# Expert passes of two sizes instead of eight, with TensorE's passes in a loop

## The chip, the cores and the metric

The kernel runs on one core of a Trainium2 chip. The metric is the device time of one execution in microseconds (us). It is one inference step of a two-layer decoder trunk, in float32 throughout, written directly for the engines with semaphores: every engine has its own instruction stream, and nothing reorders it.

## The reference, cut to what matters

288 tokens (256 of a prompt, 8 sequences of 4 new ones) go through two layers. Each layer mixes tokens by three recurrent branches and then has a feed-forward part: dense in layer 0, and a mixture of experts in layer 1. Only the latter is touched here.

```python
def swiglu(h, w1, w3, w2):
    return (jax.nn.silu(h @ w1) * (h @ w3)) @ w2

def moe_swiglu(h, router, w1, w3, w2):
    logits = (h @ router).astype(jnp.float32)
    top_v, top_i = lax.top_k(logits, TOP_K)            # 2 of 8
    probs = jax.nn.softmax(top_v, axis=-1)
    gate = jnp.sum(jax.nn.one_hot(top_i, N_EXPERTS) * probs[..., None], axis=-2)
    for e in range(N_EXPERTS):
        out = out + gate[..., e:e + 1] * swiglu(h, w1[e], w3[e], w2[e])
```

A token has 1024 features, an expert's hidden width is 2816. So 576 pairs of token and expert fall on eight experts, 72 on average.

## The kernel before, in words

**Passes.** An expert's tokens are gathered into a block of columns, and one pass multiplies this block with the expert's weights. A pass has a fixed number of columns, its cap. `CAPS` gives the caps in the order of the passes 0 to 7: 91, 88, 73, 85, 76, 82, 79, 70, together 644. The experts are ranked by how many tokens they got, on VectorE (DVE) at run time, and `PASS_OF_RANK` says which pass the expert of a rank takes; so the fullest gets 91 columns and the emptiest 70. Tokens beyond a cap go to extra passes of the last cap. Passes 0 to 6 are the fixed ones (`FIXED` = 7); pass 7 and all extra ones are turns of a loop whose count is read from a register (`passes`, L2722).

**Routing.** L2875 to L2882 make the rank (`order`), the cap of each expert (`cap_of`) and its pass (`pass_of`); after them DVE scales the gathered tokens (`take_gathered`, L2869), for which TensorE (PE) waits before pass 0. The rest of the routing runs beside pass 0.

**A pass on PE** (`expert`, L2681). First the up part: 44 slabs of weights (128 x 1024, 512 KB each, w1 and w3 in turn), each 8 matmuls in two halves of 64 rows (`narrow_products`, L454). It is a loop of five turns over eight slabs (L2685) and four slabs behind it. Then a transposed scatter matrix (L2648) and the gathering of the next pass's tokens (L2619, L2626). Then the down part, a loop of four turns (L2696), each over two output blocks of three slabs (L2661; 512, 512 and 384 KB), followed by the adding of earlier results to all 288 tokens (L2672) and transposes (L2679). ACT takes silu of the w1 product (L2744), DVE multiplies it by the w3 product (L2958), ACT takes the down products (L2748).

**PE's code.** Passes 0 to 6 are seven copies of this code, made by a Python loop, with their own caps; pass 7 is an eighth copy, inside the register loop. The two inner loops are loops of the engine in each copy. ACT and DVE have one loop of seven turns and one for the rest (L2788, L2965), and work on the whole width `CAP` in all passes.

**Loads.** SyncE's queue (SPq) issues all weight loads in one order. The up slabs have a ring of eight places (`RING`, issued at L441), the down slabs a ring of six (L2525). In each pass SPq loads the first six down slabs of that pass as the last six of the pass before are used, then up slabs 8 to 43, each when slab n - 8 is used, then the first eight up slabs of the next pass, then down slabs 6 to 23. So eight up slabs and six down slabs at most lie ready. A pass loads 44 x 512 KB and 24 down slabs, 34.6 MB in all.

**Elsewhere.** The retention stage of each layer has a PE loop of four turns over a long body (L678).

Of the kernel before, what the change touches and what calls it, by code (L numbers as in the profile page):

```python
# [19 lines left out]
ALU = mybir.AluOpType  # L20
# [17 lines left out]
FF = 2816  # L38
FT = FF // 128
NE = 8  # L40
CAP, CAP_STEP = 91, 3
FIXED = NE - 1
PASS_OF_RANK = (0, 1, 3, 5, 6, 4, 2, 7)
CAPS = [CAP - CAP_STEP * PASS_OF_RANK.index(q) for q in range(NE)]
LAST_CAP = CAPS[FIXED]
OVERFLOWS = 7
MAXP = 1 + OVERFLOWS
NFF = NE + 1
# [58 lines left out]
def constants():  # L107
# [51 lines left out]
    c["tie"] = np.tile(np.concatenate([[1e6], -np.arange(1.0, NE)]), (128, 1))  # L159
    c["pass_of_rank"] = np.tile(np.array(PASS_OF_RANK, float), (128, 1))  # L160
    off, at = 0, {}
# [59 lines left out]
def build(nc, xT_in, w_mix, w_lora, w_rank, w_gkup, vec_in, vecf_in, router_in, w_ff, s_ret, s_gla, s_rw,  # L221
# [50 lines left out]
    def settle(eng):  # L272

        eng.sem_inc(settled, 1)
# [2184 lines left out]
    def experts(nc, block, sig, layer, merge, rs):  # L2460
# [12 lines left out]
        key, above, order, cap_of, excess = w(NE), w(NE, NE), w(NE), w(NE), w(NE)  # L2473
# [25 lines left out]
        def count(p, per, k):  # L2499

            i, done = p
            return i * per + (done * per + k)
# [65 lines left out]
        def _(pe):  # L2568
# [39 lines left out]
            def keep_busy(n, unused):  # L2608

                for k in range(n):  # L2610
                    mm(unused[:, 0:T], ones, xT[:, k, :], start=True, stop=True)

            def gather_tokens(n, cap):

                pe.wait_ge(sig("picked"), n)
                for j in range(2):
                    for r in range(4):
                        rows = slice(NS * r, NS * r + NS)
                        mm(HG[r][:, CAP * j:CAP * j + cap], htok2[rows, j, :], gather[rows, 2, 0:cap], start=(j == 0),  # L2619
                           stop=False)  # L2620
                for r in range(4):
                    for j in range(2):
                        k = 4 * j + r
                        for i in range(2):
                            for c in range(2):
                                last = mm(HG[r][64 * c:64 * c + 64, CAP * j:CAP * j + cap],  # L2626
                                          htok[:, i, 128 * k + 64 * c:128 * k + 64 * c + 64], gather[:, i, 0:cap],
                                          start=False, stop=(j == 1 and i == 1))
                    last.then_inc(sig("hg_ps"), 1)

            def up(p, cap, n, turn):

                i, done = p
                s = n % RING
                per = len(range(s, UP_SLABS, RING))
                fill = fills_before(layer, s) + fills(len(STREAM), s) + done * per + n // RING + 1
                pe.wait_ge(slab_in[s], turn * 16 + (i * (per * 16) + fill * 16))
                pe.wait_ge(sig("w3_free" if n % 2 else "w1_free"), turn * (RING // 2) + count(p, FT, n // 2 + 1))
                if n in (2, 3):
                    pe.wait_ge(sig("oT"), count(p, KT, n - 1))  # L2640
                narrow_products(pe, s, bank[n % 4][:, 0:cap], hg[:, :, 0:cap])

            def scatter_matrix(p):

                pe.wait_ge(sig("gated"), count(p, 1, 1))
                pe.wait_ge(sig("w3_free"), count(p, FT, FT + 1))
                for i, (a, n) in enumerate(TILES):
                    last = nc.tensor.transpose(SC[0:CAP, a:a + n], gated[0:n, i, :], ident[0:n, 0:n])  # L2648
                last.then_inc(sig("scatter_ps"), 1)

            def down(p, cap, t, m):

                i, done = p
                pe.wait_ge(sig("oT"), t * 2 + count(p, KT, m + 1))
                for c in range(3):
                    d = 3 * m + c
                    pe.wait_ge(down_in[d], t * 16 + (i * 64 + (done * 64 + 16)))
                    n = 6 if c == 2 else KT
                    for k in range(n):
                        for h in range(2):  # L2660
                            last = mm(DOWN[m][64 * h:64 * h + 64, 0:cap], down_ring[:, d, k, 64 * h:64 * h + 64],  # L2661
                                      hid[:, KT * c + k, 0:cap], start=(KT * c + k == 0), stop=(KT * c + k == FT - 1))
                    last.then_inc(slab_done, 1)
# [12 lines left out]
            def to_tokens(p, t, m):  # L2676

                pe.wait_ge(sig("oT"), t * 2 + count(p, KT, m + 3))
                nc.tensor.transpose(OTOK[m][0:CAP, 0:128], oT[:, m, :], ident).then_inc(sig("otok_ps"), 1)  # L2679

            def expert(p, cap, next_cap):  # L2681

                pe.wait_ge(sig("hg"), count(p, 1, 1))
                settle(pe)
                with pe.Fori(0, UP_SLABS // RING) as g:  # L2685
                    for n in range(RING):
                        up(p, cap, n, g)
                for n in range(UP_SLABS // RING * RING, UP_SLABS):
                    up(p, cap, n, 0)
                scatter_matrix(p)  # L2690
                pe.wait_ge(sig("otok"), count(p, KT, 2))
                pe.wait_ge(sig("added"), count(p, KT, 2))
                gather_tokens(count(p, 1, 2), next_cap)
                pe.wait_ge(sig("w3_free"), count(p, FT, FT + 2))
                settle(pe)
                with pe.Fori(0, KT // 2) as t:  # L2696
                    for m in range(2):
                        down(p, cap, t, m)
                    for m in range(2):
                        add_up(p, t, m)  # L2700
                    for m in range(2):
                        to_tokens(p, t, m)
# [10 lines left out]
            sample_tokens()  # L2713
            keep_busy(3, bank[7])
            pe.wait_ge(sig("htok"), 1)
            gather_tokens(1, CAPS[0])
            pe.wait_ge(sig("zeroed"), 1)
            keep_busy(1, bank[3])
            for q in range(FIXED):
                expert((0, q), CAPS[q], CAPS[q + 1])  # L2720
            rest = passes(pe)
            with pe.Fori(0, rest) as i:  # L2722
                expert((i, FIXED), LAST_CAP, LAST_CAP)
            LAST = rest * KT + FIXED * KT
# [81 lines left out]
        def _(dve):  # L2806
            tt, ts, stt = nc.vector.tensor_tensor, nc.vector.tensor_scalar, nc.vector.scalar_tensor_tensor
# [3 lines left out]
            def then(ins):  # L2811

                steps[0] += 1
                ins.then_inc(sig("route"), 1)
                dve.wait_ge(sig("route"), steps[0])
# [59 lines left out]
            then(stt(out=key, in0=total, scalar=float(NE), in1=cst("tie"), op0=ALU.mult, op1=ALU.add))  # L2875
            then(tt(above, rep(key, 1, NE), column_of(key, NE), ALU.is_gt))
            then(reduce(order, above, X, ALU.add))
            ts(cap_of, order, float(-CAP_STEP), float(CAP), ALU.mult, ALU.add)
            then(tt(above, rep(cst("iota8"), 1, NE), column_of(order, NE), ALU.is_equal))
            then(tt(above, above, rep(cst("pass_of_rank"), 1, NE), ALU.mult))  # L2880
            reduce(pass_of, above, X, ALU.add)
            then(tt(excess, total, cap_of, ALU.subtract))  # L2882
            take_gathered(0)

# [4 lines left out]
            nc.vector.reciprocal(gate2[:, 0, :], den)  # L2889
            ts(turns, beyond, float(LAST_CAP), None, ALU.is_ge)  # L2890
            for c in range(1, -(-(T - LAST_CAP) // LAST_CAP)):
                then(stt(out=npass, in0=excess, scalar=float(c * LAST_CAP), in1=npass, op0=ALU.is_gt, op1=ALU.add))
                if c > 1:
                    stt(out=turns, in0=beyond, scalar=float(c * LAST_CAP), in1=turns, op0=ALU.is_ge, op1=ALU.add)
            tt(gate2[:, 1, :], gate2[:, 0, :], ex, ALU.mult)
# [5 lines left out]
            then(stt(out=move, in0=move, scalar=float(CAP), in1=cap_of, op0=ALU.mult, op1=ALU.subtract))  # L2901
            then(stt(out=turns, in0=turns, scalar=float(CAP - LAST_CAP), in1=rep(move, 1, 3), op0=ALU.mult, op1=ALU.add))
            then(tt(turns, turns, over, ALU.mult))
# [47 lines left out]
            def expert(p):  # L2951

                for f in range(FT):
                    dve.wait_ge(slab_done, count(p, FF_SLABS, FF0 + 2 * f + 2))
                    if f == 0:
                        settle(dve)
                    dve.wait_ge(sig("w1_free"), count(p, FT, f + 3))
                    tt(hid[:, f, :], bank[(2 * f + 1) % 4][:, 0:CAP], act1[:, f % 2, :],  # L2958
                       ALU.mult).then_inc(sig("w3_free"), 1)
                    choose(p, f)  # L2960
                take_gathered(count(p, 4, 4))
                for m in range(KT):
                    add_up(p, m)
# [346 lines left out]
```

## Time and profile before

| | us |
|---|---|
| median of 3 runs | 2512.42 (2511.38 to 2513.73) |
| the profiled execution, its own time | 2513.11 |
| its span, first to last instruction | 2511.3 |
| PE busy | 2442.6 (97%) |
| DVE busy | 1291.6 (51%) |
| ACT busy | 609.9 (24%) |

The profile is one execution. Its page gives the busy time of each engine, the span in 40 slices with what the DMA engines moved, the DMA queues, the chain of work that ended last, and groups of instructions by line. Its own time is 0.7 us above the median. The expert passes fill the time from about 1766 to 2498 us. A busy PE says only that matmuls were under way; whether they came as fast as they could is read from the distance between equal events.

### The profile page before, as it was taken

How to read it: one execution, taken by the hardware profiler on the slowest of the kernel's cores; microseconds unless marked ns; L12 is line 12 of the kernel's file. 1: busy time of each engine (PE TensorE's matmuls, PEld its weight loads, DVE VectorE, ACT ScalarE, POOL GpSimd, SP SyncE). 2: the span in 40 equal slices, each digit the busy share in tenths (PEclk: the TensorE clock that was granted, in tenths of full speed). 3: DMA queues.
4: the chain of work that ended last, by engine and by line, in shares of the span. 5: the costliest groups of instructions: out<-in, count | busy, mean ns of one | idle time of the engine just before them, and what ended most of it. 6: DMA issues, size and time to landing. Idle time of an engine off the chain costs nothing. (4 is left out here: it accounts for less than half of the span.)

```text
span 2511.3 us, 103490 instructions
## 1 busy us (share of the span) xinstructions
PE 2442.6 (97%) x45930; PEld 2040.3 (81%) x45930; DVE 1291.6 (51%) x3328; ACT 609.9 (24%) x1798; POOL 0.2 (0%) x4
## 2 busy tenths in 40 slices
PE   9999999999999999999999999999999999999997
PEld 7987666666699999998766666678999899888986
DVE  7666666666686676756576666667311111111111
ACT  2233333433311101233333334421111111111111
POOL 0000000000000000000000000000000000000000
PEclk9999999999999999999999999999999999999999
DMA  6334442222243454333353222234899999999997
GB/s 248 111 136 161 151 133 88 83 83 79 99 154 136 153 173 144 128 124 139 129 168 129 84 78 77 83 112 154 341 342 390 393 392 370 402 372 374 402 388 274
DMA packets 146091, 500.85 MB, mean 199 GB/s; under 512 B 18784, under 2 KB 23520, under 8 KB 143360
## 3 DMA queue, kind: packets, MB, share of 16 engines
q1 hardware_dynamic: 145792, 496.44, 54.7%
q8 instruction: 239, 3.92, 0.6%
q14 instruction: 60, 0.49, 0.1%
HBM read 476.08 MB, written 20.29 MB: 198 GB/s over the span
## 5 line engine op out<-in xcount | busy, mean ns | idle before, releaser
L301 PE MATMUL psum<-hT,ring 128*64 128x144 f32 (+1 forms) x4568 | 457.4, 346 | 3.7 <-DVE hT L2421 1.7
L454 PE MATMUL psum<-work,ring 128*64 128x91 f32 (+7 forms) x11264 | 422.0, 234 | 15.7 <-issue 7.3
L454 PEld LDWEIGHTS psum<-work,ring 128*64 128x64 f32 x11264 | 404.7, 136 | 33.3 <-issue 23.8
L301 PEld LDWEIGHTS psum<-hT,ring 128*64 128x64 f32 x4568 | 293.3, 137 | 96.2 <-issue 12.1
L2958 DVE TENSOR_TENSOR work<-psum,work 128x91 f32<-128x91 f32 x176 | 44.6, 253 | 365.4 <-PE psum L454 365.2
L2661 PE MATMUL psum<-work,proj 128*64 128x91 f32 (+7 forms) x5632 | 208.9, 234 | 10.6 <-issue 9.2
L2661 PEld LDWEIGHTS psum<-work,proj 128*64 128x64 f32 x5632 | 202.3, 137 | 16.1 <-issue 10.3
L1767 ACT ACTIVATE work<-psum 128x256 f32<-128x256 f32 (+4 forms) x320 | 104.1, 362 | 349.7 <-PE psum L1678 84.8
L301 PE MATMUL psum<-work 128*64 128x144 f32 (+4 forms) x2096 | 154.1, 282 | 4.3 <-DVE work L1258 3.6
L301 PE MATMUL psum<-y_ret,work 128*64 128x144 f32 x2400 | 156.3, 286 | 0.5 <-DVE y_ret L531 0.5
L301 PEld LDWEIGHTS psum<-y_ret,work 128*64 128x64 f32 x2400 | 148.7, 137 | 0.9 <-issue 0.9
L2949 DVE TENSOR_TENSOR xT<-xT,psum 128x288 f32<-128x288 f32 x64 | 29.1, 455 | 228.6 <-PE psum L2672 227.6
L301 PEld LDWEIGHTS psum<-work 128*64 128x64 f32 (+2 forms) x2096 | 121.3, 136 | 30.6 <-issue 11.3
L2744 ACT ACTIVATE work<-psum 128x91 f32<-128x91 f32 x176 | 43.5, 247 | 377.5 <-PE psum L454 377.5
L301 PE MATMUL psum<-y_ret,ring 128*64 128x144 f32 (+1 forms) x1280 | 126.8, 332 | 2.5 <-ACT work L1767 2.5
L301 PEld LDWEIGHTS psum<-y_ret,ring 128*64 128x64 f32 x1280 | 79.5, 137 | 18.4 <-ACT work L1767 4.5
L323 PE MATMUL psum<-hT,ring 128*128 128x288 f32 x252 | 72.8, 408 | 0.0
L2748 ACT ACTIVATE work<-psum 128x91 f32<-128x91 f32 x64 | 15.9, 248 | 228.1 <-PE psum L2661 228.1
L1563 PEld LDWEIGHTS psum<-work 64*64 64x64 f32 x1408 | 47.3, 134 | 29.4 <-issue 17.7
L546 DVE TENSOR_TENSOR y_gla<-psum,y_gla 128x288 f32<-128x288 f32 x72 | 33.0, 458 | 72.8 <-PE psum L301 72.2
L301 PE MATMUL psum<-hT,work 128*64 128x144 f32 x928 | 68.8, 287 | 0.0
L518 DVE TENSOR_TENSOR work<-ring 128x512 f32<-128x512 f32 (+1 forms) x90 | 54.7, 608 | 19.0 <-PE psum L301 19.0
(513 smaller groups left out, 3733.5 us busy)
## 6 DMA issues: line engine op xcount, KB each, us to landing
ring<-w_ff_dram SPq DMA_DIRECT2D x424, 512.0 KB, 7.3
ring<-w_mix_dram SPq DMA_DIRECT2D x256, 512.0 KB, 4.1
proj<-w_ff_dram SPq DMA_DIRECT2D x128, 512.0 KB, 5.3
proj<-w_ff_dram SPq DMA_DIRECT2D x64, 384.0 KB, 5.6
work<-s_gla_dram SPq DMA_DIRECT2D x8, 1024.0 KB, 5.3
gla_s_out<-work SPq DMA_DIRECT2D x8, 1024.0 KB, 4.7
work<-s_ret_dram SPq DMA_DIRECT2D x8, 512.0 KB, 5.4
ret_s_out<-work SPq DMA_DIRECT2D x8, 512.0 KB, 3.0
```

What stands on the lines that cost most here:

```text
L301: last = nc.tensor.matmul(out[64 * c:64 * c + 64], weights[:, 64 * c:64 * c + 64], x, start=start, stop=stop)
L323: mm = (in_halves if self.narrow else nc.tensor.matmul)(out, ring[:, s, k, :], rhs[:, k, :], start=(k == 0), stop=(k == KT - 1))
L454: mm = nc.tensor.matmul(out[64 * c:64 * c + 64], ring[:, s, k, 64 * c:64 * c + 64], rhs[:, k0 + k, :], start=(k0 + k == 0), stop=(k0 + k = ...
L518: op.tensor_tensor(s1, a21, a22, ALU.add).then_inc(sig("wsum"), 1)
L546: nc.vector.tensor_tensor(c[:, 1:3, :], two(LAST_TWO[side]), c[:, 5:7, :], ALU.add).then_inc(sig("outer"), 1)
L1563: last = mm(unit(half(W, r), c), half(AT, 1 - r)[:, c], half(X, 1 - r)[:, c], start=True, stop=True)
L1767: return nc.scalar.activation(out, in_, func, **kw)
L2661: last = mm(DOWN[m][64 * h:64 * h + 64, 0:cap], down_ring[:, d, k, 64 * h:64 * h + 64], hid[:, KT * c + k, 0:cap], start=(KT * c + k == 0) ...
L2744: ac(act1[:, f % 2, :], bank[2 * f % 4][:, 0:CAP], ACT.Silu).then_inc(sig("w1_free"), 1)
L2748: ac(oT[:, m % 2, :], DOWN[m % 2][:, 0:CAP], cp).then_inc(sig("oT"), 1)
L2949: tt(xT[:, k, :], xT[:, k, :], ADD[m % 2][:, 0:T], ALU.add).then_inc(sig("added"), 1)
L2958: tt(hid[:, f, :], bank[(2 * f + 1) % 4][:, 0:CAP], act1[:, f % 2, :], ALU.mult).then_inc(sig("w3_free"), 1)
```

## The change

The caps become two: 88 for passes 0, 2, 4, 6 and 76 for passes 1, 3, 5, 7, together 656 columns. The four fullest experts take the passes of 88, the others those of 76. The width on which ACT, DVE and the gather tables work (`CAP`) falls from 91 to 88. On PE the seven copies become a loop of three turns over two passes (88 and 76), one copy for pass 6, and the register loop for pass 7 and the rest as before. The routing gets the cap by a comparison and a multiplication, and one more small addition that must end before the next step. The loads, ACT's and DVE's loops stay as they are.

```diff
-CAP, CAP_STEP = 91, 3
+CAP, LAST_CAP, LARGE = 88, 76, 4
 FIXED = NE - 1
-PASS_OF_RANK = (0, 1, 3, 5, 6, 4, 2, 7)
-CAPS = [CAP - CAP_STEP * PASS_OF_RANK.index(q) for q in range(NE)]
-LAST_CAP = CAPS[FIXED]
+PASS_OF_RANK = (0, 2, 4, 6, 1, 3, 5, 7)
...
-            gather_tokens(1, CAPS[0])
+            gather_tokens(1, CAP)
             pe.wait_ge(sig("zeroed"), 1)
             keep_busy(1, bank[3])
-            for q in range(FIXED):
-                expert((0, q), CAPS[q], CAPS[q + 1])
+            with pe.Fori(0, LARGE - 1) as i:
+                expert((i * 2, 0), CAP, LAST_CAP)
+                expert((i * 2, 1), LAST_CAP, CAP)
+            expert((0, FIXED - 1), CAP, LAST_CAP)
             rest = passes(pe)
...
-            ts(cap_of, order, float(-CAP_STEP), float(CAP), ALU.mult, ALU.add)
+            ts(cap_of, order, LARGE - 0.5, float(LAST_CAP - CAP), ALU.is_gt, ALU.mult)
...
             reduce(pass_of, above, X, ALU.add)
+            then(ts(cap_of, cap_of, float(CAP), None, ALU.add))
             then(tt(excess, total, cap_of, ALU.subtract))
             take_gathered(0)
```

## Rows read from the trace of the kernel before

**Rows 1.** The page: span, busy time of engines, DMA in 40 slices, the up products.

```profile
span 2511.3 us, 103490 instructions
...
PE 2442.6 (97%) x45930; PEld 2040.3 (81%) x45930; DVE 1291.6 (51%) x3328; ACT 609.9 (24%) x1798; POOL 0.2 (0%) x4
...
DMA  6334442222243454333353222234899999999997
...
L454 PE MATMUL psum<-work,ring 128*64 128x91 f32 (+7 forms) x11264 | 422.0, 234 | 15.7 <-issue 7.3
```

**Rows 2.** Busy time by stretch, each from one scatter matrix to the next.

```profile
core 0: us, PE busy (x) PEld busy (x) DVE busy (x) ACT busy (x) POOL busy (x), PEclk, DMA share, GB/s
1826.70:1920.30 93.60, 92.07 (x2237) 88.23 (x2235) 13.72 (x41) 11.96 (x42) 0.00 (x0) 1.00 0.97 364
1920.30:2009.80 89.50, 87.01 (x2240) 79.70 (x2236) 13.71 (x41) 12.18 (x42) 0.00 (x0) 1.00 1.00 385
2009.80:2097.80 88.00, 86.20 (x2238) 81.55 (x2236) 13.71 (x41) 12.02 (x42) 0.00 (x0) 1.00 1.01 397
2097.80:2189.80 92.00, 87.34 (x2238) 80.57 (x2236) 13.72 (x41) 12.07 (x42) 0.00 (x0) 1.00 0.99 378
2189.80:2280.90 91.10, 85.18 (x2238) 80.63 (x2236) 13.72 (x41) 12.47 (x42) 0.00 (x0) 1.00 1.00 383
2280.90:2370.50 89.60, 87.69 (x2238) 81.21 (x2236) 13.71 (x41) 11.60 (x41) 0.00 (x0) 1.00 1.00 383
2370.50:2459.00 88.50, 83.46 (x2238) 75.93 (x2236) 13.71 (x41) 11.99 (x42) 0.00 (x0) 1.00 1.01 391
```

**Rows 3.** Timeline of ACT, passes 1 and 4: start, duration, what, [idle before].

```profile
1902.28 0.25 ACT L2744 ACTIVATE work<-psum 128x91 f32<-128x91 f32 x1 [2.18 <-PE psum L454]
...
2150.86 0.25 ACT L2744 ACTIVATE work<-psum 128x91 f32<-128x91 f32 x1 [1.86 <-PE psum L454]
...
2165.71 0.25 ACT L2744 ACTIVATE work<-psum 128x91 f32<-128x91 f32 x1 [2.32 <-PE psum L454]
...
2175.95 0.25 ACT L2744 ACTIVATE work<-psum 128x91 f32<-128x91 f32 x1 [2.32 <-PE psum L454]
```

**Rows 4.** Timeline of PE, down turns of passes 1 and 4.

```profile
1938.78 1.14 PE L2672 MATMUL psum<-work 91*64 91x288 f32 x8
...
1946.97 1.14 PE L2672 MATMUL psum<-work 91*64 91x288 f32 x8
...
2207.73 1.14 PE L2672 MATMUL psum<-work 91*64 91x288 f32 x8
...
2215.09 1.14 PE L2672 MATMUL psum<-work 91*64 91x288 f32 x8
```

**Rows 5.** Timeline of PE where it stops in passes 5, 3 and 7.

```profile
2223.86 4.91 PE L454 MATMUL psum<-work,ring 128*64 128x82 f32 x130
2230.20 4.72 PE L454 MATMUL psum<-work,ring 128*64 128x82 f32 x126 [1.43 <-issue]
2236.62 5.61 PE L454 MATMUL psum<-work,ring 128*64 128x82 f32 x149 [1.70 <-issue]
...
2107.13 3.02 PE L2661 MATMUL psum<-work,proj 128*64 128x85 f32 x77 [1.93 <-issue]
...
2469.19 3.96 PE L2661 MATMUL psum<-work,proj 128*64 128x70 f32 x74 [2.32 <-issue]
```

**Rows 6.** DMA queues: all of 140 to 229 us, then of the seven stretches.

```profile
q1 hardware_dynamic: 3406, 11.03, 34.4%
...
q1 hardware_dynamic: 68288, 241.33, 99.4%
q8 instruction: 36, 0.59, 0.4%
```

**Rows 7.** Retention loop: one turn by busy time, and its branches (first, last start).

```profile
168.00:199.10 31.10, 31.10 (x518) 27.64 (x516) 20.57 (x44) 10.76 (x21) 0.00 (x0) 1.00 0.38 135
...
L678 PEldq COMPARE_BRANCH  x8: 76/219/238, 136.3 to 1219.5; - x8
```

## The prediction

> **What bounds the kernel now.** I read the page first, then the expert passes by stretch, then single events of PE, ACT and the queues.
>
> The page [rows 1] shows PE busy for 97% of the span, so time follows PE unless PE is itself held to another's pace. The DMA line tells where that may be: it stands at 8 and 9 tenths from about 1757 us on, which are the expert passes, and far lower before. 11264 up products are 8 times 1408, so eight passes ran and no extra one.
>
> By stretch, each the down part of one pass and the up part of the next [rows 2], a stretch takes 88.0 to 93.6 us, and the DMA share is 0.97 to 1.01 in all. They carry 34.6 MB each at 364 to 397 GB/s. With 91 columns then 88 the rate is lowest and the time longest; where a small cap comes in, the rate rises and the time hardly falls. So there are two limits.
>
> ACT's silu comes once per two up slabs, so the distance of two (idle plus busy) is the pace of the up part [rows 3]. With 88 columns it is 2.18 + 0.25 = 2.43 us, with 76 at first 2.11. Later in the same pass of 76 four distances take 2175.95 - 2165.71 = 10.24 us, 2.56 each, which is 1.05 MB in 2.56 us, or 410 GB/s: the pace of the loads, reached when the slabs that lay ready are used up. A down turn takes 8.19 us with 88 columns and 7.36 with 76 [rows 4]; its 2.88 MB would take 7.0 at 410 GB/s. So: the down part follows PE at both caps; the up part follows PE at 88 and above, and for the larger part the loads at 76 and below.
>
> Third, PE stops where nothing but its code can be missing [rows 5]: 1.43 and 1.70 us within the first two turns' worth of pass 5's up part, 1.93 in the down part of pass 3, 2.32 in that of pass 7. In the seven stretches the instruction queue brought 36 blocks of 16 KB [rows 6], 5.1 per pass.
>
> **Why code is loaded once per pass.** A stretch has 2237 matmuls [rows 2]. An up turn is 8 slabs x 8 x 2 halves x 2 (each float32 product is two in the trace: 1408 for 704), 256, and runs five times; a down turn is 186 and runs four times. Written once, a pass is 2237 - 4 x 256 - 3 x 186 = 655 matmuls and as many weight loads, 1310 instructions without waits; by 5.1 blocks that is 257 per block. So the inner loops run from what PE holds, and each of the seven copies is fetched once. A down turn's branch back leaves no gap in the 7.36 us.
>
> **The change, part by part.**
>
> *Columns.* One column more costs 22 x (2.43 - 2.11) / 12 = 0.59 us in the up part, if PE sets it, and 4 x (8.19 - 7.36) / 12 = 0.28 in the down part [rows 3, 4]. The caps' sum goes up by 12. At full price that is 12 x 0.87 = 10 us; the loads' pace hides a part of it, so I build the stretches from their nearest kin [rows 2].
>
> Large down, small up (88, 76), four times: the kin are 88 then 73, 89.5 us, and 85 then 76, 92.0. The first is the low end, as its up part follows the loads for most of its length; the second with 3 x 0.28 more gives 92.8. I take the middle, 91.2.
>
> Small down, large up (76, 88), three times: 76 then 82 took 91.1; with 6 x 0.59 it is 94.6, the high end, though it holds 3.1 us of stops [rows 5], more than others. 91 then 88 took 93.6; less 15 x 0.28 it is 89.4, the low end, too low because the loads come from a pass that left them no reserve. I take 91.5, nearer to the middle than to either.
>
> Together 4 x 91.2 + 3 x 91.5 = 639.3, against 632.3 before: +7.0 (ends: 626.2 and 655.0, so -6 and +23, which would need all seven at one end). The up part of pass 0 has 3 columns less, PE's own pace: -1.8. The last down part has 6 more: +1.7. Sum of the columns: +7.
>
> *Loads.* The same 68 slabs per pass in the same order: nothing, and no gain, as neither ring grows. The waits of SPq stay.
>
> *ACT and DVE.* Widths of 88 for 91 take some 3% off operations that wait for PE anyhow (ACT idles 1.86 to 2.32 us before each silu [rows 3]): 0. The routing's new addition is one small operation, a few tenths at most, before the gathered tokens are scaled, once; no row of mine shows it, so 0 to 0.5 us, and I take 0, because it lies beside PE's gathering. If that cover fails pass 0 starts 0.3 late.
>
> *The number of passes.* From the reference's router and inputs the experts have 83, 79, 78, 72, 70, 66, 65 and 63 tokens. The first four fit 88, the others 76. So eight passes again; an extra one would be some 90 us.
>
> *Waits with registers.* In the loop PE reckons its wait values from the turn. Pass 7 does so already; and the stretch into it is one of the shortest, 88.5 us [rows 2]. 0, at most 0.1 us for each of 4 more passes.
>
> *The outer loop.* This is the new thing. Three turns over two passes make two branches back over 2 x 1310 = 2620 instructions, 10 blocks. What PE can hold: the retention loop's turn is 518 + 516 = 1034 instructions, 4 blocks [rows 7], with branches from 136.3 us and every 31.1; from 140 to 229 us, with two of them, not one instruction block came [rows 6]. So 4 blocks are held, whether 10 are no row shows. I take it that they are not, as 10 are 2.6 times the largest seen. Then each branch back finds its target gone. What a missing block costs is bounded by rows 5: PE ran at 2223.86, again at 2230.20 and again at 2236.62, 6.3 and 6.4 us apart, with 4.9 and 4.7 us of work in a block, so a block is usable 6.4 us after the one before it was begun, with the DMA engines full. Behind a branch nothing was asked for beforehand, so all 6.4 are lost, and the block after may be late again. Ends: 0 (held, or asked for early enough), and 2 x 6.4 = 12.8. I take 6.4, less the 1.4 or so that the separate copy loses at this very place: 5 net. The reserve of 8 up slabs is full then and SPq cannot load ahead, so PE's loss is not given back in the pass of 88 that follows. Twice: +10. The other blocks of a turn come as they came in the copies: 0.
>
> The Trainium skill (Runtime: NRT & Kernel Launch, "Instruction fetch mechanics") gives PE 128 KiB of instruction memory, 2048 instructions, filled in 16 KiB blocks, and says a taken branch out of a two-page window waits for a load. The 36 blocks of 16 KB agree with the block; the retention loop speaks against two pages, since it went back 4 blocks for nothing. By 2048 instructions the loop of two passes isn't held, by two pages the inner loops would have paid too. The same section calls the crossing of a block "mostly hidden"; here it is not, the stops of 1.4 to 2.3 us are of that kind.
>
> *Sum.* 2513.1 (the profiled execution's own time) + 7 + 10 = 2530.1. That execution is 0.7 above the median of the runs, so against the median I say 2529.
>
> **Rivals.**
>
> A. *PE holds all ten blocks: faster.* The branch then costs nothing, and passes 2 to 5 find their code in place and lose their stops too, some 3.5 us per pass (3.1 in the up part of pass 5, 1.9 in the down part of pass 3): -14. With the columns 2513.1 - 0.7 + 7 - 14 = 2505. It decides from a memory of 10 blocks on. For it: nothing yet seen went out of PE's memory in a loop. Against: every new copy was fetched in full, and 10 is far above 4. Chance 0.14.
>
> B. *The loads cover it: no change.* In the passes of 76 columns the loads set the pace anyhow, and if a stop falls there it is regained; if in addition the stretches come near their low ends (+1 for the columns rather than +7) and the branches cost 1 net, the time is 2514. For it: 88.0 to 89.6 us in four of the seven stretches. Against: the branch leads into a pass of 88, where PE is the slower one. Chance 0.12.
>
> C. *The jump is dearer.* The second block behind the target is late as well, 12.8 each: 2512.4 + 7 + 26 = 2545. For it: two stops in a row in pass 5. Against: in the other passes at most one of them is large. Chance 0.12.
>
> D. *It doesn't do what it says*: an extra pass, 2600 and more. Chance 0.01.
>
> **The numbers.** My forecast, 2529, has 0.61. The range reaches from 2505, to take in A's middle, to 2546. 0.2% is 5 us, about what a measurement of this kernel tells from none. Below 2507.4: 0.15, nearly all A. Within: 0.12, B. Above 2517.4: 0.73. The forecast's own range is 2518 to 2540.
>
> **What the changed kernel's profile would show.** Eight times 1408 up products. Paces of 2.43 and 2.11, then 2.56, as before. Right on the branch: two stops of 5 us or more of PE, "issue", between the last transposes of passes 1 and 3 and the first up product of passes 2 and 4, and about 36 instruction blocks still in seven stretches; under A 16 or so and no stops in passes 2 to 5. Right on the columns: stretches of 91 us on average without those two stops. The forecast is wrong if the branches leave no stop, or if stretches of 76 columns take under 88 us.

## The result, and the profile after

The changed kernel takes 2531.4 us (median of 4, 2528.9 to 2533.8) against 2513.1 for the kernel before on the same chip: ratio 1.0074, 95% interval 1.0059 to 1.0089. It is slower by 0.7%, 18 us. The forecast was 2529, the range 2505 to 2546.

The page of the kernel after, its span, its engines, the instruction queue and the up products; they answer to [rows 1]:

```profile
span 2529.3 us, 103553 instructions
...
PE 2456.1 (97%) x45930; PEld 2055.0 (81%) x45930; DVE 1288.8 (51%) x3327; ACT 608.3 (24%) x1798; POOL 0.2 (0%) x4
...
q8 instruction: 245, 4.01, 0.7%
...
L452 PE MATMUL psum<-work,ring 128*64 128x88 f32 (+1 forms) x11264 | 430.7, 236 | 23.9 <-issue 17.6
```

11264 up products again: eight passes, no extra one. PE's idle time ahead of them, put down to "issue", is 17.6 us, 7.3 before. The stretches of the kernel after, each from one scatter matrix to the next, with the columns of [rows 2]:

```profile
1825.58:1917.45 91.87, 88.84 (x2238) 82.04 (x2236) 13.52 (x41) 11.90 (x42) 0.00 (x0) 1.00 0.99 375
1917.45:2015.47 98.02, 90.59 (x2239) 86.21 (x2236) 13.52 (x41) 11.95 (x42) 0.00 (x0) 0.97 0.93 354
2015.47:2107.28 91.81, 88.15 (x2238) 81.64 (x2236) 13.52 (x41) 11.88 (x42) 0.00 (x0) 1.00 1.00 377
2107.28:2206.33 99.05, 91.27 (x2238) 86.78 (x2235) 13.52 (x41) 11.94 (x42) 0.00 (x0) 0.95 0.92 354
2206.33:2299.02 92.69, 88.28 (x2237) 81.90 (x2235) 13.52 (x41) 11.89 (x42) 0.00 (x0) 1.00 0.99 371
2299.02:2387.50 88.48, 87.92 (x2240) 83.85 (x2236) 13.53 (x41) 11.95 (x42) 0.00 (x0) 1.00 1.01 396
2387.50:2479.07 91.57, 88.40 (x2237) 81.75 (x2235) 13.53 (x41) 11.88 (x42) 0.00 (x0) 1.00 0.99 374
sum 653.49, PE 623.46 PEld 584.15 DVE 94.66 ACT 83.39 POOL 0.00; mean PE 89.06 PEld 83.45 DVE 13.52 ACT 11.91 POOL 0.00
```

Read them by kind. Large down and small up (first, third, fifth, seventh line): 91.6 to 92.7 us. Small down and large up: 98.0 and 99.1 where the loop goes back, and 88.5 in the third case, where it falls out of its last turn. The seven sum to 653.5, 21.2 more than the 632.3 before. The last stretches' ends are nearer to the end of the program than before (2529.3 - 2479.1 = 50.2, before 52.3) and pass 0 is 1 us shorter, which makes the 18.0 us between the spans.

PE's timeline at the first branch back, and the branch itself (columns: op, count, then ns least/median/most, first and last start):

```profile
1951.61 0.42 PE L2677 MATMUL psum<-table,work 128*88 128x128 f32 x2
1958.53 57.00 PE L452 MATMUL psum<-work,ring 128*64 128x88 f32 x1408 [6.51 <-issue]
...
L2717 PEldq COMPARE_BRANCH  x3: 76/6302/6322, 1951.4 to 2332.6; - x3
```

After the last transposes of pass 1 the branch takes 6.3 us and PE stands for 6.51. The third branch, which is not taken, takes 76 ns. Then PE is slow for a while. Four windows of 2 us behind the stop, and one behind the second stop, with the columns of [rows 2]:

```profile
1958.50:1960.50 2.00, 1.97 (x26) 1.97 (x27) 0.00 (x0) 0.00 (x0) 0.00 (x0) 0.50 0.00 0
1960.50:1962.50 2.00, 2.00 (x28) 1.77 (x26) 0.00 (x0) 0.24 (x1) 0.00 (x0) 0.50 0.03 8
1962.50:1964.50 2.00, 2.00 (x44) 2.00 (x42) 0.25 (x1) 0.00 (x0) 0.00 (x0) 0.73 0.69 250
1964.50:1966.50 2.00, 2.00 (x59) 2.00 (x56) 0.11 (x1) 0.24 (x1) 0.00 (x0) 1.00 0.75 246
...
2152.70:2154.70 2.00, 2.00 (x32) 2.00 (x30) 0.23 (x1) 0.00 (x0) 0.00 (x0) 0.50 0.77 248
```

At 0.50 of full clock, 1.2 GHz, PE does 26 to 28 products in 2 us, at 1.00 it does 59. It stayed low for some 5 us of work behind the first stop and 6 behind the second.

The loads stop too. Two windows of 1 us within the first stop:

```profile
1954.00:1955.00 1.00, 0.00 (x0) 0.00 (x0) 0.00 (x0) 0.00 (x0) 0.00 (x0) 1.00 1.00 402
...
1957.00:1958.00 1.00, 0.00 (x0) 0.00 (x0) 0.00 (x0) 0.00 (x0) 0.00 (x0) 0.50 0.02 9
```

The DMA engines are full until about 1955 us and nearly idle until 1962, as the rings can take no more: PE has lost the time for good. The instruction queue brought 42 blocks in the seven stretches, 36 in the kernel before.

### The profile page after: what moved, and what is told of

Its sections match the earlier page's. It is cut to its first block and busy times, and to the rows that moved or that the text cites. A ratio compares the mean times of both kernels' runs of the same rounds, so it can differ in the third digit from the quotient of the medians.

```text
span 2529.3 us, 103553 instructions
## 1 busy us (share of the span) xinstructions
PE 2456.1 (97%) x45930; PEld 2055.0 (81%) x45930; DVE 1288.8 (51%) x3327; ACT 608.3 (24%) x1798; POOL 0.2 (0%) x4
## 5 line engine op out<-in xcount | busy, mean ns | idle before, releaser
L452 PE MATMUL psum<-work,ring 128*64 128x88 f32 (+1 forms) x11264 | 430.7, 236 | 23.9 <-issue 17.6
L452 PEld LDWEIGHTS psum<-work,ring 128*64 128x64 f32 x11264 | 417.1, 137 | 38.1 <-issue 34.6
L2959 DVE TENSOR_TENSOR work<-psum,work 128x88 f32<-128x88 f32 x176 | 43.9, 250 | 383.7 <-PE psum L452 383.5
L2659 PE MATMUL psum<-work,proj 128*64 128x88 f32 (+1 forms) x5632 | 213.6, 234 | 8.4 <-issue 6.7
L2744 ACT ACTIVATE work<-psum 128x88 f32<-128x88 f32 x176 | 42.8, 243 | 397.0 <-PE psum L452 396.9
L2748 ACT ACTIVATE work<-psum 128x88 f32<-128x88 f32 x64 | 15.6, 243 | 228.5 <-PE psum L2659 228.5
```

The source lines that it names most:

```text
L452: mm = nc.tensor.matmul(out[64 * c:64 * c + 64], ring[:, s, k, 64 * c:64 * c + 64], rhs[:, k0 + k, :], start=(k0 + k == 0), stop=(k0 + k = ...
L2744: ac(act1[:, f % 2, :], bank[2 * f % 4][:, 0:CAP], ACT.Silu).then_inc(sig("w1_free"), 1)
```

## The experiments

My theory after the result: the loss is the two branches, each a load of code in the open, and the rest is small. The rival: the 12 more columns, and a new pace (2.46 us per silu at 88 columns, 2.43 before), carry it.

**Copies instead of the loop.**

```diff
-            with pe.Fori(0, LARGE - 1) as i:
-                expert((i * 2, 0), CAP, LAST_CAP)
-                expert((i * 2, 1), LAST_CAP, CAP)
-            expert((0, FIXED - 1), CAP, LAST_CAP)
+            for q in range(FIXED):
+                expert((0, q), (CAP, LAST_CAP)[q % 2], (CAP, LAST_CAP)[(q + 1) % 2])
```

> The caps of 88 and 76 as in the changed kernel, but TensorE's seven fixed passes as separate copies again. Theory (the branch back costs a load of code): both branches go, and with them 2 x 9 us (the wait of 6.3 us at the branch, and what the block behind it adds), less 1 to 2 us each for the stops that copies have there: 2516 us, and no stop of over 3 us on TensorE. Rival (the columns cost it all: 12 more, and a pace of 2.46 us instead of 2.43): nothing changes, 2529 us or more.

Measured: 2516.9 us, ratio to before 1.0010 (1.0001 to 1.0020). The theory's number to a microsecond, and the longest stop of PE is 2.48 us. Two sizes by themselves cost 0.1%; the loop costs the rest, 1.0074 against 1.0010, which is 0.64% or 16 us, with an uncertainty of some 4 from the two intervals. The seven stretches had 37 blocks of instructions, so each of the two branches of the changed kernel brought 2.5 more blocks than a copy does.

**One branch instead of two.** The loop runs two turns, passes 4 and 5 are copies.

```diff
-            with pe.Fori(0, LARGE - 1) as i:
+            with pe.Fori(0, LARGE - 2) as i:
                 expert((i * 2, 0), CAP, LAST_CAP)
                 expert((i * 2, 1), LAST_CAP, CAP)
+            expert((0, 4), CAP, LAST_CAP)
+            expert((0, 5), LAST_CAP, CAP)
```

> The loop has two turns over two passes instead of three; passes 4 and 5 are copies: one branch back instead of two. Theory: half way between the changed kernel and the one with copies alone, 2531 - 8 = 2523 us, with one stop of 6.3 us ahead of pass 2 and none ahead of pass 4. Rival (columns): 2529 us or more.

Measured: 2523.8 us, ratio 1.0037 (1.0022 to 1.0052). Its one branch took 6.1 us. So 0, 1 and 2 branches give 1.0010, 1.0037 and 1.0074: each costs 7 to 9 us, give or take 4. That the columns carry the loss, the rival, is out.

**A loop short enough.** All caps 84, as the fullest expert has 83 tokens, so that one body serves all passes; it has 1310 instructions without waits, 5.1 to 5.4 blocks.

```diff
-CAP, LAST_CAP, LARGE = 88, 76, 4
+CAP, LAST_CAP, LARGE = 84, 84, 4
...
+            with pe.Fori(0, FIXED) as i:
+                expert((i, 0), CAP, CAP)
```

> All passes with 84 columns (the fullest expert has 83), and TensorE's seven fixed passes as a loop of seven turns over one pass of 5.4 blocks of code. If TensorE holds this much: no stops in passes 1 to 6, the up part at 2.32 us and the down turn at 7.9, some 87 us per pass, in all about 2490 us. If it holds only the 4 blocks seen so far: six branches back at 8 to 9 us, 2540 us or more. If the columns alone counted (672 against 644 before, at 0.87 us each): 2537 us.

Measured: 2503.3 us, ratio 0.9955 (0.9939 to 0.9972): faster than both kernels, with 28 columns more than the kernel before. Two middle stretches of it, with the columns of [rows 2], and its queues from 1865 to 2400 us:

```profile
2182.70:2271.30 88.60, 88.30 (x2238) 84.05 (x2236) 13.29 (x41) 11.87 (x42) 0.00 (x0) 1.00 1.00 390
2271.30:2359.70 88.40, 88.06 (x2238) 83.95 (x2236) 13.29 (x41) 11.86 (x42) 0.00 (x0) 1.00 1.01 392
...
q1 hardware_dynamic: 59045, 208.59, 100.4%
```

A stretch takes 88.4 to 88.9 us in the middle, PE has hardly an idle moment, the loads run at 390 GB/s, and no instruction block comes at all: there is no line for the instruction queue. My 2490 was too low because I had 87 us for a pass. Two things are in the difference. The pace of the up part is 2.36 us per silu where I had 2.32, 0.9 us in 22 of them; and the loads take the end of each up part, at up to 2.56 us, as in [rows 3].

**The caps without the loop.** 84 everywhere, seven copies.

> 84 columns in all passes as in the loop over one pass, but TensorE's fixed passes as seven copies. It tells the caps from the loop. If the loop's gain is that its code stays with TensorE: the stops of copies come back (18 us of them in the copies of 88 and 76, 2 in the loop over one pass), less what the loads' pace covers: 2513 to 2518 us. If the equal caps gave the gain: 2503 us as the loop.

Measured: 2518.7 us, ratio 1.0020 (1.0010 to 1.0030), close to the upper end expected. The same window of its queues, its longest stop, and the sum of its seven stretches; then the same sum of the loop over one pass:

```profile
q1 hardware_dynamic: 57433, 203.25, 99.4%
q8 instruction: 32, 0.52, 0.4%
...
2107.17 3.03 PE L2659 MATMUL psum<-work,proj 128*64 128x84 f32 x77 [1.76 <-issue]
...
sum 639.64, PE 626.61 PEld 592.94 DVE 93.06 ACT 82.99 POOL 0.00; mean PE 89.52 PEld 84.71 DVE 13.29 ACT 11.86 POOL 0.00
```

```profile
sum 624.90, PE 620.29 PEld 589.25 DVE 92.97 ACT 83.03 POOL 0.00; mean PE 88.61 PEld 84.18 DVE 13.28 ACT 11.86 POOL 0.00
```

32 blocks come where the loop had none, and the stops are back. Equal caps by themselves are 0.2% slower than the kernel before; that the code stays is worth 0.65%, 16 us (1.0020 against 0.9955), of which the stretches show 14.7. PE's idle time is 8.4 us of these (13.0 against 4.6). The other 6.3 are a longer busy time of PE, with the clock at 1.00 in all stretches of both kernels; that it is the loads catching up after each stop is likely, but not shown.

**How much is held.** Three bodies of the same work, each with a part of an inner loop written out.

```diff
+                with pe.Fori(0, 2) as g:                          # 9 blocks
+                    for n in range(2 * RING):
+                        up(p, cap, n, g * 2)
...
+                with pe.Fori(0, UP_SLABS // RING - 1) as g:       # 7.4 blocks
...
+                with pe.Fori(0, KT // 2 - 1) as t:                # 6.9 blocks
```

> The loop over one pass of 84 columns with an up loop of two turns over 16 slabs instead of five over 8: the same products in the same order, but a body of 655 + 256 products with as many weight loads, 1822 instructions without waits, 7.1 to 7.4 blocks of code. How much does TensorE hold? If 8 blocks or more: as the loop of 5.4 blocks, 2503 us and no waits at the branches. If 5.4 to 7: six branches at 8 to 9 us, 2550 us.

> The loop over one pass of 84 columns with the last eight slabs of the up loop written out behind it: a body of 655 + 256 matmuls and as many weight loads, 1822 instructions without waits, 7.4 blocks. (The body of 16 slabs per turn in the run before has 655 + 512, 9.1 blocks and more, and not the 7.1 to 7.4 that its expectation says.) If TensorE holds 8 blocks: no waits at the branches, 2503 us. If it holds less than 7.4: six waits of 6 us, and the code of each pass loaded again, 2560 us or more.

> The loop over one pass of 84 columns with the last turn of the down loop written out behind it: 655 + 186 matmuls and as many weight loads, 1682 instructions without waits, some 6.9 blocks, between the body that is held (5.4) and the one that is not (7.4). If it is held: 2503 us and no waits at the branches. If not: six waits of 6 us with blocks late behind them, 12 to 14 us per branch as in the body of 7.4 blocks, 2575 to 2590 us.

Measured: 2596.1 us with 9 blocks (1.0331, 1.0314 to 1.0348), 2588.1 with 7.4 (1.0289, 1.0272 to 1.0306), 2569.9 with 6.9 (1.0222, 1.0205 to 1.0239). The first expectation miscounted its body, as the second one says. The body of 6.9 blocks came out below the 2575 to 2590 expected, with 11 us per turn and not 12 to 14. None is held. The branches of the body of 6.9 blocks and its instruction queue from 1865 to 2475 us, and PE's timeline at one of the body of 7.4:

```profile
L2724 PEldq COMPARE_BRANCH  x7: 76/5587/6744, 1864.0 to 2464.8; - x7
...
q8 instruction: 56, 0.92, 0.6%
```

```profile
1966.00 0.42 PE L2677 MATMUL psum<-table,work 128*84 128x128 f32 x2
1972.79 2.22 PE L452 MATMUL psum<-work,ring 128*64 128x84 f32 x26 [6.37 <-issue]
1975.48 4.75 PE L452 MATMUL psum<-work,ring 128*64 128x84 f32 x96 [0.48 <-issue]
```

Six branches of 5.6 us in the median (the seventh isn't taken), a stop of 6.37 us, then 26 products in 2.22 us, which is the low clock again. The queue brought 60 blocks between 1865 and 2482 us in the body of 7.4, where the body of 5.4 brings none. Against 2503.3 that is (2588.1 - 2503.3) / 6 = 14 us per turn and (2569.9 - 2503.3) / 6 = 11: the branch, the low clock, and the stops of a pass whose blocks all have to come again. The limit lies between 5.4 and 6.9 blocks; I did not narrow it.

The queue brings more than the body: 56 blocks in six turns are 9.3 per turn for 6.9, 60 are 10 for 7.4. So 2.4 to 2.6 blocks per branch come for nothing, as many as at each branch of the changed kernel. That they are blocks behind the branch, fetched ahead in case it isn't taken, would fit, and then a body and these blocks would have to find room together; no run here shows it.

**A hint for the branch.**

```diff
-            with pe.Fori(0, LARGE - 1) as i:
+            with nc.Fori(0, LARGE - 1, engines=[nc.tensor.engine], hint_back_edge=True) as i:
```

```profile
1955.45 0.42 PE L2677 MATMUL psum<-table,work 128*88 128x128 f32 x2
1956.45 1.29 PE L452 MATMUL psum<-work,ring 128*64 128x88 f32 x26 [0.59 <-issue]
1961.90 6.29 PE L452 MATMUL psum<-work,ring 128*64 128x88 f32 x104 [4.16 <-issue]
```

```profile
2331.58 3.59 PE L452 MATMUL psum<-work,ring 128*64 128x88 f32 x86
2337.61 7.62 PE L452 MATMUL psum<-work,ring 128*64 128x88 f32 x151 [2.44 <-issue]
...
L2717 PEldq COMPARE_BRANCH  x3: 85/363/386, 1955.2 to 2331.0; - x3
```

The branch itself takes 0.36 us: the target was there. PE runs 26 products and then stands for 4.16 us: the block behind the target was not. And a new stop of 2.44 us is at the exit. I take it that PE had followed the hint there instead of the code that comes next, which isn't shown. The sum comes out even. At the two branches PE stands for 4.75 us (0.59 + 4.16) and 4.08 (0.63 + 3.45), where it stood for 6.51 and 6.40: 4.1 us less. The exit costs 2.44 us and a clock of 0.50 for 3.4 us behind it, half of which is lost: 4.1 us more. Behind the two branches the clock is low as it was without the hint.

**The layout.** Rows of gathered and hidden values 91 elements apart, in the changed kernel and in the loop over one pass.

```diff
+        hg_wide, hid_wide = w(KT, 91), w(FT, 91)
+        hg, hid = hg_wide[:, :, 0:CAP], hid_wide[:, :, 0:CAP]
```

> The changed kernel with the gathered tokens and the hidden rows laid out 91 elements apart, as before the change, and not 88; the same work and columns. The up part with 88 columns had a pace of 2.43 us before and has 2.46 after. If the layout is the reason: 2.43 again in the passes of 88, 4 x 22 x 0.03 and a little in the down part, 3 to 4 us less, 2528 us. If it is not: 2531 us and 2.46.

> The loop over one pass of 84 columns with rows of tokens and hidden values 91 elements apart, not 84. The pace of the up part was 2.36 us there, where the line through 2.43 at 88 and 2.11 at 76 gives 2.32. If the layout costs it: 2.32 to 2.33 us, the down turn from 7.96 to 7.9, and 8 x 22 x 0.03 = 5 us less at most, as the loads hold the end of the up part anyway: 2498 to 2502 us. If not: 2503 us and 2.36.

Measured: 2528.1 us (1.0048, 1.0031 to 1.0064) and 2501.2 (0.9949, 0.9932 to 0.9966). ACT's silu in the loop over one pass with rows 84 apart, then with 91:

```profile
1875.96 0.24 ACT L2742 ACTIVATE work<-psum 128x84 f32<-128x84 f32 x1 [2.12 <-PE psum L452]
```

```profile
1879.50 0.24 ACT L2743 ACTIVATE work<-psum 128x84 f32<-128x84 f32 x1 [2.08 <-PE psum L452]
```

2.12 + 0.24 = 2.36 us against 2.08 + 0.24 = 2.32, and 2.46 against 2.43 in the passes of 88. The pace is a matter of layout, that is shown. What it is worth in time isn't resolved: both ratios are lower, but the intervals of each pair overlap. The last one has the lowest median, 0.5% below the kernel before.

## Why the prediction was right, point by point

*The sign and the size* were right: 2529 forecast, 2531.4 measured. The mechanism was right too. But the terms were each off, and the errors went against each other, so that the sum hit within 3 us is in part luck. In the profiles the seven stretches took 21.2 us more for the 17.0 reckoned (+7.0 and +10), pass 0 took 1.1 less for 1.8, and the tail 2.1 less where 1.7 more was reckoned: +18.0 for +16.9.

*The branches* were the mechanism, as the prediction put it: two stops, between the transposes of passes 1 and 3 and the up part of the next, of 6.51 and 6.40 us for the 6.4 reckoned from [rows 5]. To hit it this closely was luck: the stops behind such branches were 5.2 to 7.3 us long in the other runs without a hint, and the 6.4 of [rows 5] was the time from one block to the next under full DMA engines, while at the branch the DMA engines fell idle before the stop was over. That they did bears out the other half of the argument, that the reserve is full and the loss isn't given back. The term of +10 us was too small: the copies show 16. Missing was what the stop does to the clock. It fell to 0.50 in both cases, and PE worked 5 to 6 us at half speed, 2.5 to 3 us each. Rival C had a surcharge at this place, but from another cause, a late second block; PE's row behind the stop runs on for 57 us and 1408 products without a gap (in the run with one branch a gap of 0.23 us follows the first 26 products, 0.48 in the rows above of the body of 7.4). I also took off 1.4 us per branch for the stops of copies at this place; that was right about on average, as in the experiment with copies these stretches took 88.8, 89.9 and 90.9 us, and the one of the changed kernel that had neither a branch nor a stop 88.5.

*The columns* were sized at +7 us. The two sizes are worth about 2.5 together with everything else that isn't the loop (ratio 1.0010), the tail below and the new layout among it: the pace of 2.46 us for 2.43 in four up parts of 22 silus is 2.6 us by itself. The stretches of large down and small up were 91.6 to 92.7 for 91.2; those of small down and large up 88.5 to 90.9 without a branch, for 91.5. The middle between 89.4 and 94.6 was too high: its upper end came from a stretch with 3.1 us of stops.

*The tail*, +1.7 for a last pass of 76 columns, came out as -2.1. The kernel before had a stop of 2.32 us in this pass [rows 5], and what I had overlooked, a low clock behind it; the changed kernel has a stop of 1.83 us there, and the clock stays. The last pass of the kernel before, then that of the changed kernel, as windows of 29 us from the scatter matrix on:

```profile
2459.00:2488.00 29.00, 25.46 (x642) 22.99 (x640) 3.85 (x10) 3.17 (x12) 0.00 (x0) 0.94 0.93 337
```

```profile
2479.10:2508.10 29.00, 26.84 (x667) 23.50 (x667) 4.34 (x11) 3.58 (x14) 0.00 (x0) 1.00 0.97 363
```

The mean clock is 0.94 before and 1.00 after.

*Loads, ACT, DVE and waits with registers* at 0: DVE's busy time in a stretch is 13.52 us for 13.71. The routing's addition doesn't make pass 0 late: its first silu starts at 1772.26 us, before at 1772.48. The stretch behind the loop's last turn, whose waits were reckoned from registers, is the shortest of all, 88.5 us. *The number of passes* held.

*That a copy is fetched once and an inner loop isn't* is shown by the two experiments with 84 columns, 32 blocks against none. *That PE doesn't hold ten blocks* was an assumption; it is right, with a limit well below ten. The forecast of about 36 blocks in seven stretches was too low by what the branches bring for nothing: 42 came. Rival A's idea, that passes whose code stays lose their stops, is what makes the one-pass loop fast: only the body of two passes is too long for it. Rival B is out: nothing was regained in the pass of 88 behind a branch.

The Trainium skill (Runtime: NRT & Kernel Launch, "Instruction fetch mechanics") gives PE 2048 instructions, 8 blocks, and a window of two pages outside which a branch waits. The runs show that bodies of 6.9 and 7.4 blocks are loaded again and one of 5.4 isn't, so neither 8 nor 2 blocks is what a loop may count on. That does not disprove a memory of 8 blocks, as some may be taken by blocks fetched ahead.

## What to carry to other kernels

A loop on TensorE pays here if its whole body stays in the engine's instruction memory: a body of 5.4 blocks of 16 KB did, one of 6.9 did not. With 5.4 it is 16 us better than copies, whose code comes in beside full DMA queues and stops the engine. With 6.9, each turn cost 11 us: a branch of 6 us, a spell at half clock and all the blocks again. So count the instructions of a body from the trace before choosing its sizes, and rather give up exact sizes (84 columns in all passes) than the shorter body.

## What I had not expected

A stop of 6.4 us is enough to halve TensorE's clock; so was one of 2.48 us soon after one of 1.13. PE's timeline in pass 5 of the experiment with copies, and two windows behind its second stop:

```profile
2227.50 4.39 PE L452 MATMUL psum<-work,ring 128*64 128x76 f32 x126 [1.13 <-issue]
2234.37 5.82 PE L452 MATMUL psum<-work,ring 128*64 128x76 f32 x120 [2.48 <-issue]
```

```profile
2234.40:2237.80 3.40, 3.40 (x54) 3.40 (x56) 0.00 (x0) 0.25 (x1) 0.00 (x0) 0.50 0.79 322
2237.80:2245.00 7.20, 7.20 (x223) 7.20 (x222) 2.01 (x7) 0.73 (x3) 0.00 (x0) 1.00 0.89 286
```

The clock is 0.50 for 3.4 us, 54 products, where the next 7.2 us see 223. But the length of a stop doesn't settle it. The same run has a stop of 2.37 us in its last pass, where the kernel before stopped for 2.32 and fell to the low clock; here the clock stayed at 1.00 in the 29 us from the scatter matrix on:

```profile
2461.40:2490.40 29.00, 26.64 (x683) 23.97 (x681) 4.34 (x11) 3.67 (x14) 0.00 (x0) 1.00 0.97 360
```

So in such a kernel a stop may cost its length and half of the spell at 1.2 GHz behind it. The Trainium skill (TensorE: Matmul & The Clock Gate, "What's actually happening") says the gate passes half of the pulses when the engine has been idle, which the 0.50 bears out.

The distance between rows of the moving operand changes the pace of float32 products by 1 to 2% (2.36 to 2.32 us, 2.46 to 2.43), though the number of columns is the same. With 76 columns it is 2.11 us at a distance of 88 and of 91. The slower cases seen are those where the rows touch, 88 in 88 and 84 in 84. Pass 0 of the kernel before, 91 in 91, may be a third: 2.54 us, where the line through 2.11 and 2.43 gives 2.51. Why is open, and I tried no other distances.
